# Moving the start addresses of the arrays in SBUF: activations to multiples of 512 B, weights to 64 B past one

## The chip, the cores and the metric

One core of a Trainium2 chip runs the kernel. The metric is device time in microseconds; the lower, the better. The kernel before took 867.47 us (median of 3 runs, 866.96 to 868.33).

## The reference, cut to what matters

Two blocks are computed one behind the other on 256 tokens of width 1024, all in float32: first a Mamba-like SSM mixer and a latent attention (MLA) mixer, then a block with compressed, selected and windowed attention, a convolution branch, a gated feed-forward network of width 2816 and a per-layer embedding gate. Nearly all arithmetic lies in products of activations and weights:

```python
def ssd_mixer(u, in_w, ...):      proj = u @ in_w;  ...;  return y.astype(u.dtype) @ out_w
def mla_mixer(u, positions, ...): proj = u @ in_w;  q = rms_norm(c_q, ...) @ uq_w;  kv = rms_norm(c_kv, ...) @ ukv_w;  ...
h = h + (ga * y_a + gb * y_b) @ w_out[i]
v = rmsnorm(h, g_ffn[i]) @ w_up[i]
h = h + (jax.nn.gelu(v_gate) * v_val) @ w_down[i]
```

## The kernel before, in words

**Layout.** Features lie on the 128 partitions, tokens on the free axis: an activation array is a row of tiles of 128 partitions by 256 float32 (1,024 B a partition). All weights stream from DRAM in the order of use as 256 slabs of 128 partitions by 1,024 float32 (8 blocks of 128 x 128, so 512 B a partition each).

**Exact products from a fast type.** TensorE multiplies in the type `float32r`, which keeps fewer bits, so each operand is split in a high part and a low part, and each product is three matmuls (lines 628 to 630): high weights by high activations, high weights by low activations, low weights by high activations. The weight block is the stationary operand (loaded into the array by an LDWEIGHTS ahead of each matmul), the activation tile of 256 columns is the moving one. Where the output is wanted with tokens on the partitions (kinds V and C: lines 635 to 637), the activation is stationary and the weights move, 256 or 512 columns. There are 5,988 such matmuls: 5,928 with 256 moving columns, 48 with 512 and 12 with 64.

**The weight stream.** SP's queue loads slab s into `raw[:, s % 6]`. ScalarE (`feed_slabs`, line 1122) copies it, rounded, to `wh[:, s % 6]`; GpSimd (line 571) subtracts to get `wl[:, s % 6]`. TensorE waits for `wl_ready`; ScalarE may overwrite a part when TensorE is done with it. So a slab passes DMA, ScalarE, GpSimd and TensorE in turn, with six in flight.

**The rest.** VectorE takes the results out of PSUM (line 1611 scales them, line 1813 adds them to the residual, line 1809 and its likes make low parts) and does the convolution taps (lines 1719 and 1720). ScalarE makes high parts, squares and nonlinear functions. Attention work (lines 734 to 757, 846 to 875, 964 to 1022) is interleaved with projections in TensorE's program; each engine runs its own program, written out by hand, and semaphores tie them.

**Where things lie.** Each partition's SBUF is handed out in the order of the `sb` calls, from byte 16,512, and the last 105 KB are the arena, in which `ar` places the arrays of each phase at the next multiple of 32 B. Counted modulo 512 B this gives, before the change:

| array | read by TensorE as | start modulo 512 B |
|---|---|---|
| `raw`, `wh`, `wl` (all six slabs and all their blocks) | weights | 128 |
| `uh`, `ul`, `ynh`, `ynl`, `ogh`, `ogl`, `ffh`, `ffl`, `cqh`, `cql`, `ckh`, `ckl` | activations | 448 |
| `onh`, `onl`, `mh`, `ml`, `ph`, `pl`, `cxh`, `cxl` | activations | 480 |
| `cnh`, `cnl` | activations | 96 |
| `cst` (holds the identity) | operand of transposes | 0 |
| `pn` (probabilities) | operand of transposes | 64 |

Of the kernel before, what the change touches and what calls it, by code (L numbers as in the profile page):

```python
# [18 lines left out]
P = 128  # L19
T = 256  # L20
TB = T // P
DM = 1024
KD = DM // P
# [33 lines left out]
FIRST_SLABS = 2  # L57
FIRST_COLS = 8
WARM_UP = 20


def weight_jobs():
# [186 lines left out]
def vector_columns():  # L249

    at, c = {}, 0
    for name, n in [("norm0", 8), ("norm1", 8), ("final1", 8), ("sconv_w", SSM_CT * SSM_TAPS), ("sconv_b", SSM_CT),
                    ("ssm_d", 16), ("ssm_nw", 16), ("dt_bias", 1), ("a_log", 1), ("qnorm", 3), ("kvnorm", 2),
                    ("g_mix", 8), ("pos_k", 16), ("pos_v", 16), ("conv_w", CONV_CT * CONV_TAPS), ("conv_b", 4),
                    ("ln_g", 4), ("ln_b", 4), ("b_co", 8), ("g_ffn", 8), ("fconv_w", 2 * KF * FF_TAPS),
                    ("fconv_b", 2 * KF), ("g_ple", 8), ("g_final", 8)]:
        at[name] = c
        c += n
    return at, c
# [7 lines left out]
def build(nc, slabs_dram, vec_dram, const_dram, x_dram, p_dram, out_dram):  # L267
# [4 lines left out]
    VC, n_vec = vector_columns()  # L272
    ctx = ExitStack()
    with ctx:
        def sb(name, shape, dt=f32):
            return ctx.enter_context(nc.sbuf_tensor(name, shape, dt))


        raw = sb("raw", [P, RAW_RING, SLAB])
        wh = sb("wh", [P, PART_RING, SLAB], f32r)  # L280
        wl = sb("wl", [P, PART_RING, SLAB], f32r)
        h = sb("h", [P, KD, T])
        sq = sb("sq", [P, KD, T])
        vec = sb("vec", [P, n_vec])
        cst = sb("cst", [P, N_CONST])
        ident_b = sb("ident_b", [P, P], bf16)
        mask_s = sb("mask_s", [P, P], bf16)
        cmp_add = sb("cmp_add", [P, P], bf16)
        ones = sb("ones", [P, P])
        sqsum = sb("sqsum", [P, 2, T])  # L290

        msq, root, step = sb("msq", [P, 2 * TB]), sb("root", [P, 2 * TB]), sb("step", [P, 2 * TB])
        late = sb("late", [P, T])
        late_tok = sb("late_tok", [P, TB])
        root1 = sb("root1", [P, TB])
        gain12 = sb("gain12", [P, KD])
        ident = cst[:, 0:128]
        swap = cst[:, 128:256]
        cmp_ok = cst[:, 896:1024]
# [9 lines left out]
        cursor = [0]  # L309
# [3 lines left out]

        def ar(name, shape, dt=f32):
            n = int(np.prod(shape)) * 4
            t = nc.alloc_sbuf_tensor_at(name, [P] + list(shape), dt, offset=base + cursor[0])
            cursor[0] += -(-n // 32) * 32
            assert cursor[0] <= arena_kb * 1024, (name, cursor[0])
            return t


        HEADS = 4
        phase()
        uh, ul = ar("uh", [KD, T], f32r), ar("ul", [KD, T], f32r)
        after_u = cursor[0]
        ynh, ynl = ar("ynh", [16, T], f32r), ar("ynl", [16, T], f32r)
        xs, bT, cT = ar("xs", [16, T]), ar("bT", [8, T]), ar("cT", [8, T])
        acp = ar("acp", [3 * P], f32r)
        sel = ar("sel", [SSM_H], f32r)
# [119 lines left out]
        def sem(name):  # L449
            if name not in sems:  # L450
                sems[name] = ctx.enter_context(nc.semaphore(name))
            return sems[name]
# [140 lines left out]
        def _(pe):  # L593
# [103 lines left out]
            pe.wait_ge(sem("memset"), 2)  # L697
            for _ in range(WARM_UP):
                nc.tensor.matmul(PS_TR[:, 0:P], ones[:], ones[:], start=True, stop=True)
# [1643 lines left out]
```

## Time and profile before

| | |
|---|---|
| median of 3 runs | 867.47 us |
| profiled execution: its span | 865.4 us |
| TensorE matmul busy | 847.8 us (98%) |
| GpSimd busy | 624.1 us (72%) |
| VectorE busy | 526.8 us (61%) |
| ScalarE busy | 485.7 us (56%) |
| mean granted TensorE clock | 0.994 of 2.4 GHz |
| DMA | 138.46 MB, mean 160 GB/s, queue busy 51.9% |

A matmul's busy time in the profile is from its start to its modelled end, and the next starts long before that end. So the busy share says only that TensorE is never empty; how fast it goes is read from the distance between two starts. A matmul record has a duration of 0.28 us, while starts lie some 0.12 us apart.

### The profile page before, as it was taken

What the parts mean: (1) busy time and instruction counts of PE and PEld (TensorE: products, weight loads), DVE (VectorE), ACT (ScalarE), POOL (GpSimd) and SP (SyncE); (2) the same over time, 40 slices, a digit from 0 to 9 for tenths busy, and PEclk for the clock granted to TensorE, in tenths of its full rate; (3) what the DMA queues carried; (4) which work ended last, traced back from release to release, by engine and by line L of the source; (5) the groups of instructions that cost most, each with busy time, mean ns of one, the idle gap of its engine ahead of it and who ended that gap; (6) DMA issues with size and microseconds to landing.
All of it is one profiled execution on the core that took longest, in us unless ns stands there. A gap on an engine that the chain in (4) does not pass through costs nothing.

```text
span 865.4 us, 18278 instructions
## 1 busy us (share of the span) xinstructions
PE 847.8 (98%) x7055; PEld 816.2 (94%) x7055; DVE 526.8 (61%) x1543; ACT 485.7 (56%) x925; POOL 624.1 (72%) x282
## 2 busy tenths in 40 slices
PE   8999999999999999999999999999999999999995
PEld 8999988889998899999999999988999999999995
DVE  5997758883243535445458998875566676641164
ACT  6755476664446456563846457875644544554361
POOL 4899756655997455563979899455868888889680
PEclk9999999999999999999999999999999999999997
DMA  8666633332774343433566577433646666667511
GB/s 331 192 219 218 193 99 98 99 98 75 220 218 155 114 145 107 140 99 122 162 204 190 180 210 222 127 95 116 184 144 204 177 192 182 187 193 221 170 49 50
DMA packets 38678, 138.46 MB, mean 160 GB/s; under 512 B 4416, under 2 KB 4544, under 8 KB 38592
## 3 DMA queue, kind: packets, MB, share of 16 engines
q1 hardware_dynamic: 38592, 137.30, 51.9%
q8 instruction: 56, 0.92, 0.5%
q14 instruction: 30, 0.25, 0.1%
HBM read 136.23 MB, written 1.05 MB: 159 GB/s over the span
## 4 chain that ended last, share of the span: by engine, by line
PE 80%; DVE 4%; issue 2%; ACT 1%; POOLq 0%; POOL 0%; ACTq 0%; DVEq 0%
PE ps L628 22%; PE ps L629 22%; PE ps L630 21%; DVE ps L1720 1%; PE ps L850 1%; PE ps L756 1%; PE ps L673 1%; PE ps L655 1%; PE ps L637 1%; PE ps L635 1%; PE ps L636 1%; PE ps L874 1%; PE ps L983 1%; PE ps L846 1%; PE ps L821 1%
## 5 line engine op out<-in xcount | busy, mean ns | idle before, releaser
L571 POOL TENSOR_TENSOR wl<-raw,wh 128x1024 fp32r<-128x1024 f32 x254 | 606.9, 2413 | 199.1 <-ACT wh L1122 198.9
L628 PE MATMUL ps<-uh,wh 128*128 128x256 f32 (+1 forms) x1248 | 352.4, 282 | 1.9 <-POOL wl L571 0.8
L629 PE MATMUL ps<-ul,wh 128*128 128x256 f32 (+1 forms) x1248 | 348.7, 279 | 0.0
L630 PE MATMUL ps<-uh,wl 128*128 128x256 f32 (+1 forms) x1248 | 348.3, 279 | 0.0
L1122 ACT ACTIVATE wh<-raw 128x1024 fp32r<-128x1024 f32 (+1 forms) x255 | 262.9, 1052 | 85.8 <-PE ps L630 77.9
L628 PEld LDWEIGHTS ps<-uh,wh 128*128 128x128 f32 (+1 forms) x1248 | 233.8, 187 | 3.7 <-issue 1.6
L629 PEld LDWEIGHTS ps<-ul,wh 128*128 128x128 f32 (+1 forms) x1248 | 233.7, 187 | 0.0
L630 PEld LDWEIGHTS ps<-uh,wl 128*128 128x128 f32 (+1 forms) x1248 | 233.2, 187 | 0.1
L1813 DVE TENSOR_TENSOR h<-ps,h 128x256 f32<-128x256 f32 x32 | 13.6, 425 | 103.8 <-PE ps L630 103.7
L629 PE MATMUL ps<-ffl,wh 128*128 128x256 f32 x176 | 49.3, 280 | 0.0
L628 PE MATMUL ps<-ffh,wh 128*128 128x256 f32 x176 | 49.1, 279 | 0.0
L630 PE MATMUL ps<-ffh,wl 128*128 128x256 f32 x176 | 49.1, 279 | 0.0
L1720 DVE SCALAR_TENSOR_TENSOR ps<-cpad,vec,ps 128x256 f32<-128x256 f32 x120 | 48.6, 480 | 0.0
L1611 DVE TENSOR_TENSOR fraw<-ps,late 128x256 f32<-128x256 f32 x44 | 18.4, 421 | 38.7 <-PE ps L630 38.6
L1720 DVE SCALAR_TENSOR_TENSOR ps<-sraw,vec,ps 128x256 f32<-128x256 f32 x96 | 38.9, 478 | 0.0
L1720 DVE SCALAR_TENSOR_TENSOR ps<-fraw,vec,ps 128x256 f32<-128x256 f32 x88 | 38.1, 481 | 0.0
L628 PE MATMUL ps<-ynh,wh 128*128 128x256 f32 x128 | 36.1, 282 | 0.0
L628 PE MATMUL ps<-ogh,wh 128*128 128x256 f32 x128 | 36.1, 282 | 0.0
L630 PE MATMUL ps<-ynh,wl 128*128 128x256 f32 x128 | 35.8, 280 | 0.0
L629 PE MATMUL ps<-ynl,wh 128*128 128x256 f32 x128 | 35.7, 279 | 0.0
L630 PE MATMUL ps<-ogh,wl 128*128 128x256 f32 x128 | 35.7, 279 | 0.0
L629 PE MATMUL ps<-ogl,wh 128*128 128x256 f32 x128 | 35.6, 278 | 0.0
(363 smaller groups left out, 1690.8 us busy)
## 6 DMA issues: line engine op xcount, KB each, us to landing
raw<-slabs SPq DMA_DIRECT2D x255, 512.0 KB, 4.0
h<-x_fm SPq DMA_DIRECT2D x4, 256.0 KB, 4.1
out_fm<-outb SPq DMA_DIRECT2D x4, 256.0 KB, 2.2
cst<-shape_consts SPq DMA_DIRECT2D x1, 768.0 KB, 8.4
vec<-vectors SPq DMA_DIRECT2D x1, 299.5 KB, 8.6
pin<-p_fm SPq DMA_DIRECT2D x1, 256.0 KB, 3.8
raw<-slabs SPq DMA_DIRECT2D x1, 128.0 KB, 2.8
vec<-vectors SPq DMA_DIRECT2D x1, 4.0 KB, 2.4
```

The source lines that it names most:

```text
L571: nc.gpsimd.tensor_tensor(wl[:, s % PART_RING, :], raw[:, s % RAW_RING, :], wh[:, s % PART_RING, :].bitcast(f32), ALU.subtract).then_inc(s ...
L628: nc.tensor.matmul(res, w_h, a_h, start=first, stop=False)
L629: nc.tensor.matmul(res, w_h, a_l, start=False, stop=False)
L630: ins = nc.tensor.matmul(res, w_l, a_h, start=False, stop=last)
L635: nc.tensor.matmul(res, a_h, w_h, start=first, stop=False)
L636: nc.tensor.matmul(res, a_h, w_l, start=False, stop=False)
L637: ins = nc.tensor.matmul(res, a_l, w_h, start=False, stop=last)
L655: ins = nc.tensor.matmul(PS_M[:, n.col + c:n.col + c + 1], src[:, b * P:(b + 1) * P], ones[:, 0:1], start=n.summed or k == g * per, stop=n ...
L1122: nc.scalar.activation(wh[:, s % PART_RING, 0:n], raw[:, s % RAW_RING, 0:n], ACT.Copy)\
L1611: tt(dst, o[0:rows, 0:T], late[0:rows, :], ALU.mult).then_inc(sem("dve_evac"), 1)
L1720: return stt(dst, src, w, dst, ALU.mult, ALU.add)
L1813: tt(h[:, k, :], o[:, 0:T], h[:, k, :], ALU.add).then_inc(sem("dve_evac"), 1)
```

## The change

It changes where arrays lie and nothing else: no instruction is added, removed or put in another order, and all shapes stay. The small arrays (`vec`, `msq`, `root`, `step`, `late_tok`, `root1`, `gain12`) are allocated first; a filler tensor then moves `raw` to 64 B past a multiple of 512 B, and with it `wh` and `wl` (their sizes are multiples of 512 B). A second filler puts `h` and `sq` on a multiple of 512 B, a third `ones`, `sqsum`, `late` and, behind them, the arena. Inside the arena each array of at least 512 B starts at a multiple of 512 B, and each of 256 to 511 B at a multiple of 256 B. Afterwards the weights stand at 64 modulo 512 B, all the activation arrays of the table above at 0, `cst` at 0 and `pn` at 0. Rows of `cpad`, `sraw` and `fraw`, which are 1,144, 1,036 and 1,032 B long, keep only their first row on a boundary; TensorE doesn't read them.

```diff
+PIECE = 512
+STATIONARY_AT = 64
...
+        def start_at(offset):
+
+            gap = (offset - nc.sbuf_base) % PIECE
+            if gap:
+                sb(f"gap{nc.sbuf_base}", [P, gap // 4])
+
+        vec = sb("vec", [P, n_vec])
+        msq, root, step = sb("msq", [P, 2 * TB]), sb("root", [P, 2 * TB]), sb("step", [P, 2 * TB])
+        late_tok = sb("late_tok", [P, TB])
+        root1 = sb("root1", [P, TB])
+        gain12 = sb("gain12", [P, KD])
+        start_at(STATIONARY_AT)
         raw = sb("raw", [P, RAW_RING, SLAB])
         wh = sb("wh", [P, PART_RING, SLAB], f32r)
         wl = sb("wl", [P, PART_RING, SLAB], f32r)
+        start_at(0)
         h = sb("h", [P, KD, T])
         sq = sb("sq", [P, KD, T])
-        vec = sb("vec", [P, n_vec])
         cst = sb("cst", [P, N_CONST])
...
+        start_at(0)
         ones = sb("ones", [P, P])
         sqsum = sb("sqsum", [P, 2, T])
-
-        msq, root, step = sb("msq", [P, 2 * TB]), sb("root", [P, 2 * TB]), sb("step", [P, 2 * TB])
         late = sb("late", [P, T])
-        late_tok = sb("late_tok", [P, TB])
-        root1 = sb("root1", [P, TB])
-        gain12 = sb("gain12", [P, KD])
...
         def ar(name, shape, dt=f32):
             n = int(np.prod(shape)) * 4
+            if n >= PIECE // 2:
+                cursor[0] += -cursor[0] % (PIECE if n >= PIECE else PIECE // 2)
             t = nc.alloc_sbuf_tensor_at(name, [P] + list(shape), dt, offset=base + cursor[0])
```

## Rows read from the trace of the kernel before

**Rows 1.** The page's parts 1 and 2: busy us, share, instructions; slices of the span.

```profile
PE 847.8 (98%) x7055; PEld 816.2 (94%) x7055; DVE 526.8 (61%) x1543; ACT 485.7 (56%) x925; POOL 624.1 (72%) x282
PEclk9999999999999999999999999999999999999997
```

**Rows 2.** Busy time by stretch: start:end, length, engines, clock, DMA, GB/s.

```profile
10.00:50.00 40.00, 38.43 (x324) 37.95 (x323) 36.70 (x93) 28.05 (x46) 34.98 (x15) 1.00 0.76 258
450.00:500.00 50.00, 50.00 (x431) 50.00 (x430) 44.49 (x105) 25.88 (x35) 42.11 (x18) 1.00 0.59 180
660.00:820.00 160.00, 160.00 (x1360) 160.00 (x1360) 82.19 (x215) 77.46 (x110) 136.04 (x57) 1.00 0.64 192
```

**Rows 3.** TensorE's timeline, 426 to 437 us: start, duration; matmuls with `og` moving.

```profile
425.77 0.28 PE L629 MATMUL ps<-ogl,wh 128*128 128x256 f32 x1
...
436.95 0.28 PE L628 MATMUL ps<-ogh,wh 128*128 128x256 f32 x1
```

**Rows 4.** The same, 402 to 413 us.

```profile
401.89 0.28 PE L629 MATMUL ps<-ogl,wh 128*128 128x256 f32 x1
...
413.00 0.28 PE L628 MATMUL ps<-ogh,wh 128*128 128x256 f32 x1
```

**Rows 5.** The same, 612 to 623 us, with `mh` and `ml` moving.

```profile
611.73 0.28 PE L628 MATMUL ps<-mh,wh 128*128 128x256 f32 x1
...
622.89 0.29 PE L628 MATMUL ps<-mh,wh 128*128 128x256 f32 x1
```

**Rows 6.** Durations (ns min/median/max) by line and tile, in those three stretches and of transposes.

```profile
L628 PE MATMUL ps<-ogh,wh x69: 279/279/317, 415.7 to 439.8; 128*128 128x256 f32 x69
L628 PE MATMUL ps<-ogh,wh x34: 276/276/363, 401.7 to 413.0; 128*128 128x256 f32 x34
L628 PE MATMUL ps<-mh,wh x64: 279/282/286, 611.7 to 634.4; 128*128 128x256 f32 x64
L863 PE MATMUL ps<-cst,pn x3: 272/272/273, 302.3 to 302.5; 128*128 128x128 f32 x3
```

**Rows 7.** TensorE's timeline, three transposes merged in one row.

```profile
302.30 0.49 PE L863 MATMUL ps<-cst,pn 128*128 128x128 f32 x3
```

**Rows 8.** TensorE's timeline, 525.1 to 526.1 us: matmuls with only 64 columns.

```profile
525.15 0.28 PE L629 MATMUL ps<-hgl,wh 128*128 128x64 f32 x1
...
526.04 0.28 PE L628 MATMUL ps<-hgh,wh 128*128 128x64 f32 x1
```

**Rows 9.** TensorE's timeline, 266 to 267.5 us: matmuls with 512 columns.

```profile
266.00 0.39 PE L636 MATMUL ps<-wl,ckh 128*128 128x512 f32 x1
...
267.40 0.39 PE L636 MATMUL ps<-wl,ckh 128*128 128x512 f32 x1
```

**Rows 10.** Who waited for whom, longest first: engine line waited for, us, times, longest.

```profile
PE ps L673 <- DVE root L1572: 2.5, 1, 2.5
PE ps L1089 <- ACT sq L1135: 1.9, 1, 1.9
PE ps L699 <- DVE sraw L1653: 1.1, 1, 1.1
```

**Rows 11.** Groups by line: line, engine, tiles, shape, count | busy us, mean ns | idle.

```profile
L571 POOL TENSOR_TENSOR wl<-raw,wh 128x1024 fp32r<-128x1024 f32 x254 | 606.9, 2413 | 199.1 <-ACT wh L1122 198.9
...
L1122 ACT ACTIVATE wh<-raw 128x1024 fp32r<-128x1024 f32 (+1 forms) x255 | 262.9, 1052 | 85.8 <-PE ps L630 77.9
...
L1720 DVE SCALAR_TENSOR_TENSOR ps<-cpad,vec,ps 128x256 f32<-128x256 f32 x120 | 48.6, 480 | 0.0
...
L1720 DVE SCALAR_TENSOR_TENSOR ps<-sraw,vec,ps 128x256 f32<-128x256 f32 x96 | 38.9, 478 | 0.0
```

**Rows 12.** DMA issues: tensors, queue, count, KB each, us from issue to landing.

```profile
raw<-slabs SPq DMA_DIRECT2D x255, 512.0 KB, 4.0
```

## The prediction

> **What bounds the kernel.** I read the page's busy shares first: matmuls cover 98% of the span, at full granted clock in every slice but the last [rows 1]. TensorE is the bound; nothing else passes 72%. The list of waits then says that TensorE hardly waits for anyone: the longest entry is 2.5 us [rows 10]. So the time is the number of matmuls times the distance between their starts, and a change that removes no instruction can act only on that distance.
>
> That distance is read from the timeline. I used three stretches without a gap, all with 256 moving columns and all at full clock.
>
> - 426 to 437 us: 96 rows, 95 steps from 425.77 to 436.95, so 11.18/95 = 117.7 ns [rows 3]. The moving tile starts at 448 modulo 512 B, the weights at 128.
> - 402 to 413 us: the same arrays at the same places, 98 steps from 401.89 to 413.00, so 113.4 ns [rows 4].
> - 612 to 623 us: moving tile at 480, which is not a multiple of 64; 93 steps in 11.16 us, 120.0 ns [rows 5].
>
> 256 columns at 2.4 GHz are 106.7 ns. The surplus is 11, 7 and 13 ns for one and the same work. The records' durations move with it: 279, 276 and 282 ns, against 272 ns for the transposes of line 863, whose operands stand at 0 and 64 [rows 6]. So something in the array's supply of data costs 4 to 10 ns a matmul, and it depends on more than the shape. Addresses seem one part of it, 480 against 448 [rows 3, 5], but not all: the same addresses give two distances 4.3 ns apart [rows 3, 4]. I take it for two read streams of TensorE, the moving tile and the next weight load, that get in each other's way at certain distances and then keep one of several rhythms. The long stretch shows the common one: 1,360 matmuls in 160 us, 117.6 ns [rows 2].
>
> **The sum.** All weight matmuls but 60 have 256 columns: 5,928. Of these, 5,741 start less than 130 ns behind their predecessor; read start by start their mean distance is 117.60 ns, together 675.2 us. The others follow a wait or a matmul of another kind, and I leave them alone.
>
> *Term 1, the 256-column matmuls.* What could the distance fall to? The low bound is the weight load. Where the matmul has only 64 columns, it can't be the limit, and starts still lie 0.89 us over 8 steps apart, 111 ns, read to the nanosecond 111.7 [rows 8]. That is what loading 128 x 128 weights takes, each time, here with the weights at 128. The transposes could speak for less, (0.49 - 0.272)/2 = 109 ns a step [rows 6, 7], but they come three at a time, and right behind an idle weight path. The high bound is that nothing happens or that it gets worse, 120.0 [rows 5]. Between 111.7 and 120.0 I take 111.7: at 0 and 64 the streams start in other places than in any of the three stretches, no operand crosses a 64 B boundary, and line 863, the row at just these places, shows the shortest duration of all. Gain: (117.60 - 111.7) x 5,741 = 33.9 us.
>
> *Term 2, 512 columns.* 45 steps of 233.3 ns (six steps in 1.40 us) [rows 9] against 213.3 ns of columns. If half of the surplus goes, 0.5 us. Bounds 0 and 0.9.
>
> *Term 3, other matmuls.* The attention's float32 matmuls and transposes pass the array at half speed, in short groups. Their places change too. I put them at 0, with bounds of 1 us gained or lost, from 48 transposes and some 200 others at up to 5 ns.
>
> *Term 4, what is given back.* With TensorE 5% faster, others have less room. VectorE is busy 36.7 of 40 us between 10 and 50 us and 44.5 of 50 us between 450 and 500 [rows 2]; shortened by 5% these stretches hold 38.0 and 47.5 us, so VectorE fills 97% and 94% of them, and its order is fixed. I charge 1.5 us, with bounds of 0 and 4. GpSimd takes 2.41 us a slab [rows 11]; TensorE will take 24 x 111.7 = 2.68 us, so GpSimd stays hidden with 0.27 us to spare. It is the next bound: from 2.7 us a slab it would set the pace. ScalarE's copy is 1.05 us [rows 11]. A slab's DMA lands in 4.0 us with six slabs in flight [rows 12] and stays hidden.
>
> *Edits at nothing.* VectorE's taps take 480 ns from `cpad` (rows at 448, 56, 176, 296 modulo 512) and 478 from `sraw` [rows 11], so VectorE doesn't care where a row starts; bounds of both signs 0.2%, which its idle time covers. The fillers and the small columns in front cost no instruction. The first loads are the same transfers in the same order. The waits at the end (line 1089) [rows 10] stay.
>
> Sum against the profiled execution: 865.4 - 33.9 - 0.5 + 0 + 1.5 = 832.5 us. The median of the runs is 2.1 us above that execution's span, so 834.6, rounded 835.
>
> **Where the trace and a rule of the Trainium skill part.** Its page "SBUF — State Buffer", section "Who interferes with whom", says that PE and ACT never wait on anyone, and "TensorE: Matmul & The Clock Gate", section "Step-by-step: what each phase is for", that a weight load takes nothing from the running matmul's reads, since each has its own port. By these the start address can't matter and the change gives 0. The traces disagree with it as far as they go: three distances for one shape, all at full clock [rows 3 to 5]. The formula of the latter page's section "Back-to-back issue gap" (N/2.4 + 2.5) gives 109.2 ns for 256 columns; by it the surplus of 8.4 ns over 5,741 matmuls would be 48 us, and the page names nothing that could cause it.
>
> **Rivals.**
>
> 1. *All in the short rhythm.* The new places only make sure that TensorE keeps the short rhythm [rows 4]. For it: that rhythm is in the trace, for 98 steps on end. Against: it is reached at the old places too, so the places needn't be what selects it. (117.60 - 113.4) x 5,741 = 24.1 us; given back 1: 865.4 - 24.1 - 0.3 + 1 + 2.1 = 844.
> 2. *Freer than the weight load.* The 111.7 ns hold only for weights at 128; at 64 a step is 109 ns, as between the transposes [rows 7]. Gain (117.60 - 109.0) x 5,741 = 49.4 us, given back 3 (GpSimd then has 24 x 109 = 2.62 us a slab): 865.4 - 49.4 - 0.5 + 3 + 2.1 = 821.
> 3. *Nothing.* The rhythm comes from somewhere else (which wait came last before a run of matmuls), and 117.6 stays: 866 to 868. For it: two distances at one placement [rows 3, 4]. Against: 480 instead of 448 costs 2.3 ns [rows 3, 5].
> 4. *Slower.* Now the weight stream stands 64 B ahead of the moving stream at the start, and the moving one reads 1,024 B in the time in which the load reads 512. It runs into the load at once, at each matmul. If this is a worse distance than the present 192 B, the step is 120.0 ns [rows 5] or more: (120.0 - 117.6) x 5,741 = 13.8 us, 865.4 + 13.8 + 2.1 = 881. It decides from a distance above 117.9 ns on. For it: a placement can be worse [rows 5]; against: part of that row is the start off the 64 B grid, which the change does away with.
>
> **How the numbers follow.** Chances: forecast 0.33, short rhythm 0.25, freer 0.10, nothing 0.19, slower 0.13. The likeliest gives 835, with a range of its own of 830 to 840 (its terms' bounds). Leaving out a part of the freer case and the slower case, the range is 818 to 868. A measurement of this kernel can tell 0.2%, 1.7 us, from no change: faster 0.69 (the first three and a bit of the fourth), same 0.17, slower 0.14.
>
> **What would show it.** In the profile after, the timeline between 620 and 780 us gives the step at once: 111.7, 113.4, 109, 117.6 or 120. The durations of line 628's records should fall from 279 to at most 276 ns, if the stall is gone. The feed-forward stretch, where nothing else can hold TensorE, must show the whole gain per matmul; if it does and the total doesn't, term 4 is wrong, and the waits of TensorE for VectorE (line 1611, line 1720) or GpSimd (line 571) will have grown. The mean of line 571 must stay near 2.41 us and that of line 1720 near 480 ns. I am wrong altogether if the distance stays at 117.6 ns at the new places.

## The result: 859.24 us, 1.2% faster and far less than forecast

The changed kernel took 859.24 us (median of 4 runs, 851.05 to 860.67) against 867.82 us; ratio 0.9882, 95% interval 0.984 to 0.9923. Forecast were 835 us and a range of 818 to 868. The direction is right; the gain is 8.6 us where 33 were forecast. New is the scatter: the four runs of the kernel before lie within 1.4 us (those beside the experiments within 4), the changed one's spread over 10. In all 16 timed runs of it, those of the experiments included, it took between 850.84 and 861.11 us, median 854.5.

The profiled execution is the shortest of the first four (span 849.3 us). Its page, parts 1 and 5, stands against [rows 1, 11]:

```profile
PE 830.9 (98%) x7055; PEld 798.9 (94%) x7055; DVE 528.2 (62%) x1543; ACT 485.6 (57%) x925; POOL 623.0 (73%) x282
...
L583 POOL TENSOR_TENSOR wl<-raw,wh 128x1024 fp32r<-128x1024 f32 x254 | 605.8, 2416 | 185.5 <-ACT wh L1134 185.3
...
L1732 DVE SCALAR_TENSOR_TENSOR ps<-cpad,vec,ps 128x256 f32<-128x256 f32 x120 | 48.7, 483 | 0.0
```

The other engines' instructions cost what they cost (GpSimd 2,416 against 2,413 ns, the taps 483 and 478 against 480 and 478). Only TensorE's matmul time fell, by 17 us. TensorE's timeline, three stretches of the changed kernel (start us, duration, instruction), the first and last row of each:

```profile
39.82 0.28 PE L642 MATMUL ps<-uh,wl 128*128 128x256 f32 x1
...
50.89 0.28 PE L640 MATMUL ps<-uh,wh 128*128 128x256 f32 x1
...
397.80 0.28 PE L642 MATMUL ps<-ogh,wl 128*128 128x256 f32 x1
...
408.90 0.28 PE L641 MATMUL ps<-ogl,wh 128*128 128x256 f32 x1
...
605.84 0.28 PE L640 MATMUL ps<-mh,wh 128*128 128x256 f32 x1
...
616.94 0.28 PE L642 MATMUL ps<-mh,wl 128*128 128x256 f32 x1
```

94 steps in 11.07 us are 117.8 ns, 98 steps in 11.10 us are 113.3 ns, and the third again 98 in 11.10, 113.3 ns. So the two rhythms of before, 117.8 and 113.4 [rows 3, 4], are still the only ones. What changed is how often each comes, and that the 120.0 ns of the `mh` stretch [rows 5] are gone. Read start by start, 93% of the steps of before were 116 ns or longer; in this execution 30% are. The mean of all of them fell from 117.60 to 114.67 ns: 2.93 x 5,733 = 16.8 us, and the 512-column steps, 229.5 instead of 233.3 ns, give 0.2. The span fell by 16.1.

The durations go with it. The changed kernel's line 640 (ns min/median/max), first from 640 to 680 us, then from 30 to 60:

```profile
L640 PE MATMUL ps<-uh,wh x118: 276/276/276, 640.0 to 679.7; 128*128 128x256 f32 x118
...
L640 PEld LDWEIGHTS ps<-uh,wh x86: 192/192/192, 29.9 to 60.0; 128*128 128x128 f32 x86
L640 PE MATMUL ps<-uh,wh x85: 281/281/281, 30.0 to 59.7; 128*128 128x256 f32 x85
```

### The profile page after: what moved, and what is told of

Same layout as the page of the kernel before. It is cut to its first block, busy times and chain, and to the rows that moved or that the text cites. A ratio compares the mean times of both kernels' runs of the same rounds, so it can differ in the third digit from the quotient of the medians.

```text
span 849.3 us, 18278 instructions
## 1 busy us (share of the span) xinstructions
PE 830.9 (98%) x7055; PEld 798.9 (94%) x7055; DVE 528.2 (62%) x1543; ACT 485.6 (57%) x925; POOL 623.0 (73%) x282
## 4 chain that ended last, share of the span: by engine, by line
PE 80%; DVE 2%; ACT 2%; issue 2%; POOL 1%; POOLq 0%; ACTq 0%; DVEq 0%
PE ps L640 21%; PE ps L642 21%; PE ps L641 21%; PE ps L862 1%; POOL wl L583 1%; PE ps L768 1%; PE ps L647 1%; PE ps L649 1%; PE ps L648 1%; PE ps L667 1%; PE ps L685 1%; PE ps L886 1%; ACT wh L1134 1%; PE ps L858 1%; PE ps L995 1%
## 5 line engine op out<-in xcount | busy, mean ns | idle before, releaser
L583 POOL TENSOR_TENSOR wl<-raw,wh 128x1024 fp32r<-128x1024 f32 x254 | 605.8, 2416 | 185.5 <-ACT wh L1134 185.3
```

The costliest lines, as they stand in the source:

```text
L583: nc.gpsimd.tensor_tensor(wl[:, s % PART_RING, :], raw[:, s % RAW_RING, :], wh[:, s % PART_RING, :].bitcast(f32), ALU.subtract).then_inc(s ...
```

## The experiments

**m1: the grid.** The theory to test was that the places of the two read streams decide, against the phase at the start and against contention with other engines. The core of the kernel of matmuls alone (comments and "..." added):

```diff
+for mv in range(0, 128, 16):            # elements of 4 B: steps of 64 B
+    for st in range(0, 128, 16):
+        out.append((mv, st, kind, 8))   # kind A: from idle; B: behind two float32 matmuls
...
+w_h = wh[:, kk * P + st:kk * P + st + P]
...
+a_h = uh[:, kk * T + mv:kk * T + mv + T]
...
+nc.tensor.matmul(res, w_h, a_h, start=k == 0, stop=False)
+nc.tensor.matmul(res, w_h, a_l, start=False, stop=False)
+ins = nc.tensor.matmul(res, w_l, a_h, start=False, stop=k == mms - 1)
```

> A kernel of its own: it leaves out the whole model and only runs 256 groups of 24 float32r matmuls (256 moving columns) with a weight load ahead of each, as the projections have them, at all 64 pairs of start addresses (moving and weights each at 0, 64, ..., 448 modulo 512 B), each pair four times: twice from an idle TensorE, twice behind two float32 matmuls. No other engine works meanwhile. Theory 1 (the places decide): the distance of starts is a function of the pair; 448/128 gives 117.8 ns in nearly all four groups, 0/64 gives 113.3. Theory 2 (the start's phase decides, placement is by the way): every pair gives both 113.3 and 117.8 ns, and which of them comes changes from group to group at one pair. Theory 3 (contention with the other engines or DMA): with those idle the distance is 109 to 111.7 ns everywhere.

TensorE's timeline of that kernel; the first pair of rows is from distance 0 (moving 0, weights 0), the second from distance 64:

```profile
20.33 0.28 PE L348 MATMUL ps<-uh,wl 128*128 128x256 f32 x1
...
21.05 0.28 PE L348 MATMUL ps<-uh,wl 128*128 128x256 f32 x1
...
22.05 0.28 PE L348 MATMUL ps<-uh,wl 128*128 128x256 f32 x1
...
24.43 0.28 PE L348 MATMUL ps<-uh,wl 128*128 128x256 f32 x1
```

Six steps in 0.72 us are 120 ns; 21 in 2.38 us are 113.3. Mean steps of all groups, over the last 17 steps of each and sorted by distance (start of the weights minus start of the moving tile, modulo 512 B), 32 groups each:

```
distance   steps in ns (groups)
  0        119.6 to 120.0 (31)                  256   119.4 to 120.0 (32)
 64        113.3 to 113.4 (25), 117.8 (7)       320   113.3 to 113.4 (24), 117.8 (8)
128        118.4 to 119.0 (31), 120.1 (1)       384   118.4 to 119.1 (31), 120.1 (1)
192        117.7 to 117.8 (29), 113.3 (3)       448   117.7 to 117.8 (31), 113.4 (1)
```

(One group of distance 0 ran at half the clock, at the start.) Theory 1 holds with one correction: only the distance of the two starts counts, and it counts modulo 256 B. Theory 2 holds within a distance: 64 and 192 have two rhythms, and the start draws one. Theory 3 falls: all other engines idle, the steps are the model's.

**e1: the changed kernel again.**

> The changed kernel once more, to see how its times spread. If the rhythm of a stretch is drawn anew in each execution, times scatter between 851 and 861 us again, in lumps; a profile shows the feed-forward stretch (1,556 matmuls without a break) wholly at 113.3 or wholly at 117.8 ns, 6.9 us apart. If the 851 us was an outlier of another cause, all lie at 859 to 861.

853.27 to 860.67 us, median 856.27, ratio 0.9871 (0.9847 to 0.9896). The profiled execution took 856.1 us, 6.8 more than the first. Busy time by stretch (start:end, length, engines), 660 to 800 us, the first row from the changed kernel's first execution, the second from this one:

```profile
660.00:800.00 140.00, 140.00 (x1238) 140.00 (x1237) 74.50 (x194) 72.16 (x102) 126.67 (x54) 1.00 0.66 200
```

```profile
660.00:800.00 140.00, 140.00 (x1191) 140.00 (x1191) 74.19 (x194) 69.97 (x98) 121.44 (x52) 1.00 0.65 193
```

1,238 matmuls in 140 us against 1,191, the pace of the kernel before [rows 2]. The feed-forward stretch of 1,556 matmuls without a break is wholly in one rhythm or the other, and 1,556 x 4.44 ns = 6.9 us is the difference of the two executions. The expectation held.

**e2 and e3: half the change each** (comments added).

```diff
+        sb("gap1", [P, 112])                      # e2: raw, wh, wl to 64 modulo 512 B
         raw = sb("raw", [P, RAW_RING, SLAB])
...
+        sb("gap2", [P, 16])                       # and the rest back where it was
         h = sb("h", [P, KD, T])
```

```diff
+        sb("gap", [P, (-nc.sbuf_base) % 512 // 4])     # e3: the arena to a multiple of 512 B
         arena = sb("arena", [P, arena_kb * 256])
...
+            if n >= 256:
+                cursor[0] += -cursor[0] % (512 if n >= 512 else 256)
```

> The kernel before with only raw, wh and wl moved from 128 to 64 modulo 512 B; the activations stay at 448, 480 and 96. Theory 1 (distance between the two streams decides): the distance weights minus activations becomes 128 B instead of the 192 of before and the 64 of after; something between, 860 to 867. Theory 2 (only the activations off the 64 B grid cost, rest by chance): 866 to 868, no change.

> The kernel before with only the arena's arrays moved to multiples of 512 B (activations at 0); the weights stay at 128 modulo 512 B. If leaving the odd starts (480 and 96) is one term, it gives (120.0 - 117.8) x 285 = 0.6 us at least, up to 1.9 us if these stretches fall in the short rhythm. If a moving start at 0 is what makes the short rhythm common, the whole gain of 8 to 9 us is here; if the weights' place is, 865 to 867.

Each half alone makes the kernel slower, by the same amount: 873.59 us (ratio 1.0073, 1.0058 to 1.0087) and 873.66 us (1.0071, 1.0058 to 1.0084). All expectations missed. The reason is in m1's table, whose figures came with them: both halves put the distance at 128 (64 - 448 and 128 - 0 modulo 256). In both the mean step is 118.7 and 118.6 ns. The gain belongs to neither array's place.

**e4, e5 and e7: other distances with all activations at 0.** The edit is one number:

```diff
-STATIONARY_AT = 64
+STATIONARY_AT = 0        # e4; 192 in e5, 320 in e7
```

> The changed kernel with the weights at 0 instead of 64 modulo 512 B, all else as changed: distance 0. By the grid (119.6 to 120.0 ns at distance 0) the step rises by (119.9 - 117.6) x 5,741 = 13 us over the kernel before: 881. If only starting on the grid counted, 857 as in the changed kernel.

> The changed kernel with the weights at 192 modulo 512 B: the distance of the kernel before (192), but all activations at 0. If the distance alone decides, the feed-forward stretch is at 117.8 ns and the time is that of before less what the 480 and 96 starts cost there, 865 to 868. If the starts at multiples of 512 B have a part of their own, 855 to 862.

> The changed kernel with the weights at 320 instead of 64 modulo 512 B. If the distance counts modulo 256 B, this is the changed kernel again: 853 to 861. If it counts modulo 512, it is another kernel, and 866 to 880 would be as likely.

e4 took 879.32 us (1.013, 1.0115 to 1.0145). Of e4, the busy time by stretch, to be held against the 1,360 matmuls of before [rows 2], and line 642 (660 to 800 us), against the 279 and 276 ns of [rows 6]:

```profile
660.00:820.00 160.00, 160.00 (x1335) 160.00 (x1335) 85.70 (x224) 77.90 (x111) 135.99 (x58) 1.00 0.63 191
...
L642 PE MATMUL ps<-uh,wl x309: 283/283/283, 660.0 to 770.9; 128*128 128x256 f32 x155
```

e5 took 866.5 us (0.9983, 0.9973 to 0.9994): the distance of the kernel before gives its time but for 1.5 us. In the profiles 0.9 us of that is in the step, most of it in the `mh` stretch (299 matmuls at 119.8 ns before, at 117.8 in e5) and the one from 500 us (118.1 and 117.0); the rest isn't explained. e7 took 852.91 us (0.9846, 0.9815 to 0.9878), the changed kernel's time. All three as the distance modulo 256 B says. The executions that were profiled, in one table (the step is the mean of some 5,740 steps read from the starts; "from the step" is its difference to 117.60 times their number, the last column the span's difference to 865.4; k2 has a wait of its own, of which below):

```
kernel            distance   step ns   from the step   span
e4                   0       119.86       +13.0        +12.0
e2                 128       118.68        +6.2         +5.6
e3                 128       118.64        +6.0         +5.4
e5                 192       117.45        -0.9         -1.2
changed (e1)        64       115.88        -9.9         -9.3
e7                 320       114.86       -15.7        -14.4
changed (first)     64       114.67       -16.8        -16.1
e6, below           64       114.59       -17.3        -16.0
f2, below           64       116.22        -7.9         -6.0
k1, below       64 and 192   113.92       -21.1        -19.6
f1, below       64 and 192   113.93       -21.0        -19.7
k2, below       64 and 192   113.95       -20.9        -12.6
```

**m2 and m3: can a rhythm be forced, and is there a shorter one?** The low operands got a distance of their own, so that two of three weight loads run at one distance and the third at another (comments added).

```diff
-                out.append((mv, st, kind, 8))
+                out.append((mv, mv + d, mv, mv + d, kind, 8))   # d in steps of 16 B
+                out.append((0, d1, 0, d2, kind, 8))             # two distances
```

> The kernel of matmuls alone again (it leaves out the model). Part one: the distance weights minus moving tile in steps of 16 B from 0 to 240, with the moving tile at 0 and at 32 modulo 512 B, four groups each. Part two: the low operands get a distance of their own (0, 64, 128 or 192 B), so that of three weight loads two run at the first distance and one at the second, eight groups for each of the 16 mixes. [...] If the two rhythms of distance 64 are kept by the regularity of the stream, a mix such as 64 with 192 or 128 falls in one rhythm always; a mean of its two parts, (2 x 113.3 + 118.5)/3 = 115.1, would say that each load is slowed for itself.

> The kernel of matmuls alone (it leaves out the model). Part one: mixes in 16 B steps of the low distance with the high distance at 48, 64, 80 or 208 B, four groups each, to see whether any goes below 113.3 ns. If 113.3 ns (272 cycles of 2.4 GHz) is the floor of a float32r pair with 256 columns, none does; if it is only the best on the 64 B grid, some mix gives 109 to 112. Part two: 64, 128 and 192 moving columns at distances 0, 64, 128 and 192: here the weight load is the longer of the two. If the load's own time doesn't depend on its place, 64 and 128 columns give 111.7 ns at all four, which is the low bound that the prediction took; if placement stops the load too, the four differ.

In m2 the distances between multiples of 64 B gave means of 116.6 to 123.7 ns, and not always a value between their neighbours' (118.6 to 118.9 at 80). 113.3 showed at 64 (5 of 8 groups) and at 192 (1 of 8) alone. A moving tile at 32 gave at distance 64 the same as one at 0 (3 and 2 of 4 groups), so what costs is the distance, not the tile's place. Distance 160 gave 119.8 to 120.2: that is the distance of the `mh` stretch before the change (128 - 480 modulo 256), and its 120.0 ns [rows 5]. A mix of 64 with 128 gave 118.1 to 118.6, not the 115.1 of each load slowed for itself. Of the 16 mixes one went to 113.3 ns in all 8 groups, after at most 13 matmuls of transition: 64 with 192. 192 with 64 did in 4 of 8, and 64 with 0 never (117.8 in all). m3 added 64 mixes in steps of 16 B, four groups each: none below 113.3, and only 64 with 192 (4 of 4) and 64 with 64 (3 of 4) reach it. With 192 moving columns, where the load is the longer, the last groups run as here (timeline of m3, distance 128):

```profile
305.58 0.27 PE L350 MATMUL ps<-ul,wh 128*128 128x192 f32 x1
...
307.92 0.27 PE L350 MATMUL ps<-ul,wh 128*128 128x192 f32 x1
```

21 steps in 2.34 us, 111.4 ns; distances 64 and 192 gave 111.6 and 111.7. The groups at distance 0 with 192 columns, one at 64, and nearly all with 64 and 128 columns, ran wholly or partly at the 1.2 GHz level of the clock and tell nothing; four groups of 64 columns at distance 0 and full clock gave 111.65. So the weight load's own 111.7 ns, the low bound of the prediction, was right at these places, but pairs with 256 columns don't get there.

**k1 and k2: the mix in the model.**

```diff
+LOW_AT = 192
...
         wh = sb("wh", [P, PART_RING, SLAB], f32r)
+        start_at(LOW_AT)
         wl = sb("wl", [P, PART_RING, SLAB], f32r)
```

> The changed kernel with the low weights (wl) at 192 modulo 512 B instead of 64, all else as changed: two of three weight loads at distance 64, the third at 192. In the kernel of matmuls alone this mix fell into the short rhythm in 8 of 8 groups, within 4 to 13 matmuls. If the rhythm is a property of the two read streams alone, every long stretch runs at 113.3 ns here too, the mean step falls from 115.9 or so to 114.0 and the time to 867.9 - (117.6 - 114.0) x 5,741 / 1000 = 847 us, with little scatter (under 2 us). If other engines' work disturbs the rhythm, some stretches stay at 117.8 and the time is 851 to 861 as in the changed kernel. The kinds V and C have the mix turned round (192 and 64), which gave 118.9 in four of eight groups, at most 1 us.

> The version with wl at 192 once more, beside the changed kernel on the same chip. Its six times lay in two lumps, 847.5 to 849.9 and 855.0 to 855.2, as far apart as the feed-forward stretch in its two rhythms (1,556 steps x 4.44 ns = 6.9 us). If that is the cause, two lumps come again, and a profile of a run near 855 has this stretch at 117.8 and all else as before. Median 848 to 855.

> The changed kernel beside it: 851 to 861, median 857 as before; 3 to 7 us slower than the version with wl at 192, since that one has nearly all other stretches in the short rhythm and this one has half.

k1 took 852.44 us (0.983, 0.9803 to 0.9857), k2, the same kernel again, 848.12 us (0.977, 0.9757 to 0.9783); beside it on the same chip the changed kernel took 852.14 us (0.9835, 0.9804 to 0.9865). The mix beats both kernels. But 4 of its 12 times lie at 854.6 to 855.2 and the others at 847.5 to 849.9, so k1's "little scatter" missed. I had put that on the feed-forward stretch, and k2's profiled execution, one of the longer ones (852.8 us), refutes it: that stretch runs at 1,238 matmuls in 140 us there too. From k2, the busy time of that stretch and TensorE's longest wait (sum in us, count, longest):

```profile
660.00:800.00 140.00, 140.00 (x1238) 140.00 (x1237) 77.37 (x202) 72.64 (x103) 126.77 (x54) 1.00 0.65 200
...
PE ps L642 <- DVE sraw L1625: 5.1, 1, 5.1
```

VectorE's timeline of k2 (start, duration):

```profile
83.06 9.07 DVE L1762 TENSOR_TENSOR acp<-acr,acp 32x384 fp32r<-32x384 f32 x1
```

and GpSimd's, 80 to 93 us, its slabs that follow each other without a gap in one row:

```profile
77.59 14.13 POOL L585 TENSOR_TENSOR wl<-raw,wh 128x1024 fp32r<-128x1024 f32 x6
```

One VectorE instruction with both inputs in SBUF, 0.55 us in the kernel before, takes 9.07 us, and ends 0.41 us behind GpSimd's six slabs on end (77.59 + 14.13 = 91.72 us). VectorE's queue stands, TensorE waits 5.1 us, and its granted clock is at the 1.2 GHz level (0.50) from 92 to 96 us. In the table above that is k2's span, 7 us longer than k1's at the same step. The kernel before has a gap ahead of each slab at this point (GpSimd's timeline, in brackets the wait and what ended it):

```profile
82.97 2.41 POOL L571 TENSOR_TENSOR wl<-raw,wh 128x1024 fp32r<-128x1024 f32 x1 [0.41 <-ACT wh L1122]
85.80 2.45 POOL L571 TENSOR_TENSOR wl<-raw,wh 128x1024 fp32r<-128x1024 f32 x1 [0.41 <-ACT wh L1122]
```

That is what the Trainium skill's page "SBUF — State Buffer", section "Who interferes with whom", says of a VectorE instruction with two SBUF inputs beside a GpSimd one that reads SBUF: the second to come is kept out. The trace agrees, and shows more: in k2 it was kept out to the end of the fourth GpSimd instruction, not of one. A gap between slabs isn't needed for it to come in, though. In k1 GpSimd runs thirteen slabs on end (68.44 to 99.64 us), and still VectorE's instruction ends after 2.08 us (k1, VectorE's timeline and one slab of GpSimd's):

```profile
83.36 2.08 DVE L1762 TENSOR_TENSOR acp<-acr,acp 32x384 fp32r<-32x384 f32 x1
...
84.97 2.75 POOL L585 TENSOR_TENSOR wl<-raw,wh 128x1024 fp32r<-128x1024 f32 x1
```

It ends at 85.44, 0.41 us behind the end of the slab that it met (85.04), and the next slab takes 2.75 instead of 2.4 us. In e6's profile (the changed kernel) it ends 0.41 us behind the second slab's end, after 3.87 us. So in the three late cases it comes in where one slab ends, the first, the second or the fourth; why it misses some of these ends stays open.

**f1, f2 and f3: that instruction with one operand in PSUM.**

```diff
-nc.scalar.activation(acp[0:SSM_H, :], acr[0:SSM_H, :], ACT.Copy).then_inc(sem("decay_hi"), 1)
+link(nc.scalar.activation(acp[0:SSM_H, :], acr[0:SSM_H, :], ACT.Copy))
+nc.scalar.activation(PS_M[0:SSM_H, 0:3 * P], acp[0:SSM_H, :].bitcast(f32), ACT.Copy)\
+    .then_inc(sem("decay_hi"), 1)
...
-tt(acp[SSM_H:2 * SSM_H, :], acr[H, :], acp[H, :].bitcast(f32), ALU.subtract)\
+tt(acp[SSM_H:2 * SSM_H, :], acr[H, :], PS_M[H, 0:3 * P], ALU.subtract)\
```

> The version with wl at 192, with one edit more: ScalarE writes the high part of the decay rows to PSUM too, and VectorE's subtraction for acp reads it there, so it has only one operand in SBUF. Theory (VectorE's instruction with two SBUF operands is kept out while GpSimd's slabs follow each other without a gap): it takes 0.6 us in every execution, the lump at 855 is gone, and all times lie at 846 to 849. If the lump has another cause, it comes again in a third to a half of the runs.

> The same edit in the changed kernel. What is left of its scatter is then the rhythm: times near 850 (feed-forward stretch at 113.3) or near 857 (at 117.8), with 1 to 3 us between for shorter stretches; nothing above 858. If the rhythm wasn't a cause, all at 850 to 852.

> The same edit in the kernel before, whose GpSimd has a gap of 0.4 us behind each slab at that point: no change, 867 to 869.

f1 took 847.49 us (five runs, 847.41 to 849.2; ratio 0.9775, 0.9762 to 0.9787). GpSimd's timeline of f1, 70 to 100 us:

```profile
68.29 28.47 POOL L585 TENSOR_TENSOR wl<-raw,wh 128x1024 fp32r<-128x1024 f32 x12
```

and VectorE's:

```profile
83.21 0.54 DVE L1764 TENSOR_TENSOR acp<-acr,ps 32x384 fp32r<-32x384 f32 x1
```

GpSimd runs twelve slabs on end, right across VectorE's 83.21 us, and the subtraction takes 0.54 us. In k1's profiled execution it took 2.08 us, in k2's 9.07. The upper group of times is gone; from 4 in 12, chance alone would leave it out of five runs with (8/12)^5 = 0.13, so the count doesn't prove it and the instruction's duration is the stronger evidence. f3 took 867.78 us (1.0003, 0.9994 to 1.0011): nothing to gain where VectorE's instruction starts in a gap. f2 took 851.03 to 861.15 us, median 854.03 (0.9862, 0.983 to 0.9894): the changed kernel's scatter stays, so it isn't this collision, although that also occurs there (3.87 us in e6's profile). "Nothing above 858" missed: in f2's profiled execution (859.4 us) the mean step is 116.22 ns; besides the feed-forward stretch the runs of matmuls from 27, 70, 412 and 597 us are in the long rhythm too.

## Why the prediction was wrong, step by step

- **What bounds the kernel, and that only the distance of starts can change:** right. Where no new wait stands in between, the span's change follows the step's change within 2 us from -21 to +13.
- **Two read streams that meet, with several rhythms:** right as far as it can be seen. m1 shows that the distance of the two starts sets the step with all other engines idle; that the reads themselves get in each other's way is the reading of it, since no record shows a read. But "addresses seem one part of it, 480 against 448" was read too coarsely: what counts is the distance of both starts modulo 256 B, 64 being best, then 192, 128 and 0. I had the difference 192 for before and 64 for after in hand and used it only for the slower rival, where I argued that 64 B ahead must collide at once. It is the best distance on the grid. Nor was the start at 480 off a 64 B grid a cost of its own, as rival 4 had it: those tiles stood at distance 160, and m2 gives 120 ns there with the tile at 0 as well.
- **Term 1, "between 111.7 and 120.0 I take 111.7": the step that failed.** I took the weight load's own 111.7 ns as what remains once the streams don't meet. At no distance of m1 and in no mix of m2 and m3 does a steady stream of 256-column pairs go below 113.3 ns; whether the streams still meet there or something else sets it, no run tells. And the gain doesn't come for all matmuls: at distance 64 each stretch draws a rhythm and keeps it, and in the executions profiled 30% of the steps stayed long (27% in e6, 57% in e1, 64% in f2, which has f1's edit too). Worth (117.60 - 114.67) x 5,733 = 16.8 us in the first execution, 17.3 in e6 and 9.9 in e1, not 33.9. The row that I leaned on, line 863 at 0 and 64, is a transpose of 128 columns; that its duration was short said nothing of pairs with 256.
- **Rival 1 (all in the short rhythm, 844) and rival 3 (nothing):** the truth is a mix of both, drawn per stretch. Rival 1's objection, that the rhythm is reached at the old places too, was right as far as it went: at 192 it comes in 4 of 64 groups of m1, at 64 in 49 of 64. Its 844 us was nearly reached, by another placement: f1 took 847.5 us at a mean step of 113.93, not 113.4.
- **Rivals 2 and 4:** refuted for this placement. 4's price was nearly right for a distance of 0: forecast +13.8 us, e4 +12.0 by the spans.
- **Term 2:** 0.5 forecast, 0.2 measured. **Term 3** was not separated; the sum leaves less than 1.5 us for it and term 4 together.
- **Term 4, given back:** 1.5 forecast, 0.9 by the sum of the first profile. But its mechanism was the wrong one. Not VectorE's busy share but one instruction's access to SBUF cost time, since GpSimd has fewer gaps between slabs when TensorE is faster: 7 us in k2's profiled execution, and by their times, which is not shown, in 4 of the 12 of k1 and k2.
- **Edits at nothing:** held; VectorE's and GpSimd's means moved by under 1%.

Open is what draws the rhythm at the start of a stretch. In m1 both came from idle and behind other matmuls alike, and in two executions of one program the same stretch differs, so it is something finer than the program's order.

## What to carry to other kernels

In a TensorE-bound stream of weight load and matmul, read the distance of starts to the nanosecond in a stretch without gaps, and try the distance between the starts of the two operands modulo 256 B: it moved this kernel between 848 (k2) and 879 us (e4) with no instruction changed. Change both arrays' places together; here each half alone cost 0.7%. When the bound engine gets faster, look for VectorE instructions with two SBUF inputs beside a GpSimd that no longer pauses; f1's operand in PSUM is a remedy.

## What the runs showed of the hardware

Steady steps of float32r matmuls of 256 columns with a weight load each, at 2.4 GHz: 113.3 or 117.8 ns at distance 64, 117.8 (seldom 113.3) at 192, 118.4 to 119.1 (seldom 120.1) at 128, 120.0 at 0, period 256 B, with all other engines idle. 113.3 ns are 272 cycles. The long rhythm has two forms with the same step: matmuls of 279 to 280 ns with loads of 187 to 188 before the change, 281 after it, where the loads of one line in three take 192 and the others 187 to 188. For 512 moving columns (44 steps a kernel, all with `ck`; the activation is the stationary operand there) the order of the distances is another: 233.4 and 233.5 ns at 64 (before, e5), 232.6 and 232.3 at 128 (e2, e3), 229.3 at 192 (the changed kernel), 227.9 at 0 (e4). A VectorE subtraction of 32 x 384 elements with both inputs in SBUF lasted 0.55 us in a gap of GpSimd's and 2.08, 3.87 or 9.07 where slabs followed each other, by how many of their ends it missed.
